# Last expert pair combined on chip by one-hot products, the other rows reloaded behind the last weights, and a reordered beginning

## What is computed

```python
for i in range(2):
    mod = silu(c) @ w_ada[i] + b_ada[i]              # 6 vectors of 1024, for both token groups
    x = x + mod[2] * mixer_i(rmsnorm(x, norm_mix[i]) * (1 + mod[1]) + mod[0])
    h = rmsnorm(x, norm_ffn[i]) * (1 + mod[4]) + mod[3]
    # each token goes to 2 of 32 experts (top group of 4, then top 2 of its 8), with gates g0, g1
    y = sum(g_c * (silu(h @ w_gate[e_c]) * (h @ w_up[e_c])) @ w_down[e_c] for c in (0, 1))
    x = x + mod[5] * y
out = rmsnorm(x, norm_final)
```

## Time and profile before

| what | before |
|---|---|
| median of three runs | 1372.38 us (1372.12 to 1373.4) |
| profiled execution: own time, span of its instructions | 1375.31 us, 1373.4 us |
| PE busy, DVE busy, ACT busy, POOL busy | 1208.0, 451.8, 329.9, 200.1 us |
| mean granted TensorE clock | 0.953 |
| DMA moved | 336.90 MB, mean 245 GB/s |
| chain that ended last | PE 68%, DMA 18%, DVE 6%, ACT 3%, POOL 2%, issue 2% |

### The profile page before, as it was taken

How to read it: one execution, slowest core, us unless ns; L and a number is a source line. 1 busy time by engine, 2 the same in 40 slices (tenths; PEclk the granted TensorE clock), 3 DMA queues, 4 the chain that set the end, 5 groups by cost and what they waited for, 6 DMA issues and landing times.

```text
span 1373.4 us, 16614 instructions
## 1 busy us (share of the span) xinstructions
PE 1208.0 (88%) x6373; PEld 679.4 (49%) x6373; DVE 451.8 (33%) x973; ACT 329.9 (24%) x843; POOL 200.1 (15%) x261
## 2 busy tenths in 40 slices
PE   3999998999989999959999774999888959989774
PEld 2456654554545554446555332753554446545431
DVE  1442078543238750331111104112364331111105
ACT  4112364300123200321111104213353321111103
POOL 1000012200124510011212101052001011212100
PEclk9999999999999999979999996999999979999996
DMA  9896510576920137369999996860314469999983
GB/s 338 307 386 228 184 31 1 197 266 222 359 78 1 62 127 266 103 232 420 419 415 420 419 373 227 304 64 0 138 63 140 178 231 420 420 418 420 419 371 148
DMA packets 94386, 336.90 MB, mean 245 GB/s; under 512 B 12769, under 2 KB 16583, under 8 KB 69618
## 3 DMA queue, kind: packets, MB, share of 16 engines
q1 hardware_dynamic: 73472, 303.18, 56.7%
q0 software_dynamic: 13952, 25.86, 6.8%
q10 hardware_dynamic: 6897, 6.97, 1.5%
HBM read 333.76 MB, written 23.18 MB: 260 GB/s over the span
## 4 chain that ended last, share of the span: by engine, by line
PE 68%; DMA 18%; DVE 6%; ACT 3%; POOL 2%; issue 2%; SPq 0%; ACTq 0%; DVEq 0%; POOLq 0%
PE bank L856 60%; DMA ring<-in_moe_w_down_dram 11%; PE bank L860 5%; DMA ring<-in_moe_w_up_dram 3%; PE bank L887 3%; DMA arena<-expert_rows 1%; DMA xR<-in_x_sample_dram 1%; POOL ring L2671 1%; POOL hT L2674 1%; PE bank L953 1%; ACT ring L1976 1%; DMA hT<-rows,scr 0%; POOL arena L2674 0%; DMA arena<-in_hy_freq_dram 0%; ACT rstd L1604 0%
## 5 line engine op out<-in xcount | busy, mean ns | idle before, releaser
L856 PE MATMUL bank<-ring,arena 128*64 128x256 f32 (+3 forms) x2624 | 440.3, 440 | 45.8 <-DMA ring<-in_moe_w_up_dram 17.2
L856 PEld LDWEIGHTS bank<-ring,arena 128*64 128x64 f32 (+1 forms) x2624 | 218.1, 146 | 232.4 <-issue 120.0
L856 PE MATMUL bank<-hT,ring 128*128 128x384 f32 (+4 forms) x960 | 302.7, 474 | 4.3 <-ACT hT L1676 3.6
L856 PEld LDWEIGHTS bank<-hT,ring 128*128 128x128 f32 (+1 forms) x960 | 179.2, 194 | 123.8 <-issue 16.6
L856 PE MATMUL bank<-arena 128*64 128x256 f32 (+7 forms) x800 | 118.0, 385 | 10.5 <-DVE arena L2459 4.5
L2486 DVE TENSOR_TENSOR hT<-hT,bank 128x256 f32<-128x256 f32 x32 | 13.5, 421 | 266.1 <-ACT hT L1863 266.1
L856 PEld LDWEIGHTS bank<-arena 128*64 128x64 f32 (+4 forms) x800 | 60.1, 151 | 52.3 <-issue 29.0
L1863 ACT ACTIVATE hT<-bank 128x256 f32<-128x256 f32 x32 | 12.3, 383 | 247.7 <-PE bank L856 247.7
L860 PEld LDWEIGHTS bank<-cst,hT 128*128 128x128 f32 x368 | 47.4, 190 | 48.1 <-issue 35.9
L860 PE MATMUL bank<-cst,hT 128*128 128x128 f32 x368 | 61.1, 301 | 11.4 <-DMA hT<-rows,scr 11.4
L860 PE MATMUL bank<-cst,arena 128*128 128x128 f32 (+3 forms) x207 | 32.6, 307 | 40.0 <-ACT arena L1617 23.4
(11 more groups left out here) (312 smaller groups left out, 1126.4 us busy)
## 6 DMA issues: line engine op xcount, KB each, us to landing
ring<-in_moe_w_up_dram SPq DMA_DIRECT2D x28, 2048.0 KB, 21.1
ring<-in_moe_w_down_dram SPq DMA_DIRECT2D x28, 2048.0 KB, 20.0
ring<-in_w_ada_dram SPq DMA_DIRECT2D x24, 2048.0 KB, 15.0
ring<-in_moe_w_gate_dram SPq DMA_DIRECT2D x24, 2048.0 KB, 21.1
ring<-in_ev_w_in_dram SPq DMA_DIRECT2D x11, 2048.0 KB, 11.7
arena<-in_moe_w_gate_dram SPq DMA_DIRECT2D x8, 2048.0 KB, 14.4
ring<-in_ev_w_out_dram SPq DMA_DIRECT2D x4, 2048.0 KB, 16.8
arena<-in_moe_w_up_dram SPq DMA_DIRECT2D x4, 2048.0 KB, 20.7
```

The source lines that it names most:

```text
L856: return nc.tensor.matmul(out, lhsT, rhs, start=start, stop=stop_, skip_group_check=True)
```

## The change

At the end of each expert stage step 15 is neither stored nor reloaded. A second table `gtb` (72 more products beside `tbl`) gives the gate of each slot; POOL takes the column of the last step and builds three diagonal matrices of the choice 0 gates (`diag0`); DVE builds `last_pick`, a 128 by 384 matrix that has a slot's gate in its token's column. PE then forms for each tile and half `diag0[t] @ yg[t]` plus `last_pick @ ob` in one bank (`last`, 12 products of 128 by 512), which replaces ACT's `weigh`. Since some rows of `expert_rows` are now never written, SP fills all of them with zeros beforehand (`k_zero`, four copies DRAM to DRAM ahead of the first `wout` load). On PE `down` of step 14 and the four `gff` products move ahead of `gate_up` of step 15, and down 14 is loaded to `ahead[2]`, ahead of gate 15. `row_loads` waits for the stores up to step 14 alone, and the `od` loads no longer wait for `yg2`. ACT measures tile 2 before it modulates tile 0.

At the beginning the two condition rows are loaded and transposed first, the wait at `k == 1` goes, the first `xbc` block is loaded in two halves with two `w_ada` blocks between them, and PE's work is reordered: a `w_ada` block before the parameter rows, the second half of the token transposes after the first sums, and `first_x` started after each 128-row chunk (`FIRST_MOD`, `first_taken`).

```diff
...
+FIRST_MOD = {"act": [(c, t) for c in range(4) for t in (0, 2)], "dve": [(c, 1) for c in range(4)]}
...
+    job(("cond",), "act")
     for g in range(2):
         job(("adaw", 0, g), "none", ("ada", 0, g), ADA_BANK)
+        if g == 0:
+            for i in range(5):
+                job(("par", i), "act")
+            for t in range(NT):
+                job(("xn", "mix0", t, 0), "first")
         job(("adaw", 0, g + 2), "act", ("ada", 0, g + 2), ADA_BANK)
         job(("ada", 0, g + 2), "dve", None, ADA_BANK)
+        if g == 0:
+            for t in range(NT):
+                job(("xn", "mix0", t, 1), "first")
...
+                job(("gff", l, v, h), "weighed", None, (0, 1, 7, 2)[2 * v + h])
+        for t in range(NT):
+            for h in range(2):
+                job(("last", l, t, h), "dve", None, (3, 4, 5, 6, 3, 4)[2 * t + h])
...
+                sp.wait_ge(done, JOB[("gtb", l)] + 1)
...
-                with sp.Fori(4, r - 1) as i:
...
-                next_load(l, 2 * r - 3, 2 * r - 1, 1, PAIRS - 1, 2)
+                m = 2 * r - 4
+                for part in range(2):
+                    next_load(l, m, m + 2, 0, PAIRS - 2, part)
+                next_load(l, m - 1, m + 1, 1, PAIRS - 3, 2)
+                sp.wait_ge(S("down_done%d" % l), len(PLACES[2]))
+                sp.dma_start(halves(expert_place(2, 2)), expert_source(l, PAIRS - 2, 2)).then_inc(expert_sem(l, 2, 2), 16)
+                for part in range(2):
+                    next_load(l, m + 1, m + 3, 1, PAIRS - 1, part)
+                next_load(l, m + 1, m + 3, 1, PAIRS - 1, 2)
...
-                for b in range(2):
-                    sp.wait_ge(S("stored%d_%d" % (l, b)), 16 * r)
+                even, odd = sp.to_reg(16 * r), sp.to_reg(16 * r - 16)
+                sp.wait_ge(S("stored%d_0" % l), even)
+                sp.wait_ge(S("stored%d_1" % l), odd)
...
+            first_k = LOAD_AT[("xbc", 0)]
             for k in range(n1 - 1):
-                if k == 1:
-
-                    sp.wait_ge(S("rows_in"), 16 * sum(len(t) for t in ROWS))
-                    sp.wait_ge(S("small_in"), 16 * 2)
-                static_load(k, False)
+                if k == first_k:
+                    sp.dma_start(block_view(LOADS[k])[:, 0:4, :], block_source(LOADS[k])[:, 0:4, :]).then_inc(S("first_x_in"), 16)
+                else:
+                    static_load(k, False)
+                if LOADS[k + 1] == ("wout", 0):
+                    for l in range(2):
+                        for c in range(2):
+                            sp.dma_start(outs_d[l][c * T:(c + 1) * T, :], K["k_zero"]).then_inc(S("blank"), 16)
+                if k == LOAD_AT[("ada", 0, 3)]:
+                    sp.dma_start(block_view(("xbc", 0))[:, 4:8, :], block_source(("xbc", 0))[:, 4:8, :])\
+                        .then_inc(S("full%d" % first_k), 16)
...
-                sp.wait_ge(S("yg%d" % (NT - 1)), 16)
...
+            pe.wait_ge(S("cond_in"), 16 * 2)
+            ps = open_bank("cond")
+            tr(ps[:, 0:2 * KD], prow[0:2 * KD, 0, :]).then_inc(done, 1)
+            pe.wait_ge(S("silc"), 1)
+            first_ada_block(0, 0)
+            pe.wait_ge(S("rows_in"), 16 * (sum(len(t) for t in ROWS) - 2))
...
-            for h in range(2):
-                for t in range(NT):
-                    ps = open_bank("xn", "mix0", t, h)
-                    pe.wait_ge(S("xn%d" % h), t + 1)
-                    for c in range(4):
-                        last = tr(ps[:, cols(c)], xn["mix0"][:, t, cols(4 * h + c)])
-                    last.then_inc(done, 1)
-            pe.wait_ge(S("silc"), 1)
+            for t in range(NT):
+                first_scaled(t, 0)
+            first_ada_block(2, 1)
             pe.wait_ge(S("small_in"), 16 * 2)
...
+            first_ada_sums(0)
+            for t in range(NT):
+                first_scaled(t, 1)
+            pe.wait_ge(S("first_x_in"), 16)
             for c in range(4):
                 if c == 3:
-                    first_ada(1)
+                    first_ada_block(1, 0)
+                    first_ada_block(3, 1)
...
+                down(n - 1, 0, 2)
                 pe.sem_inc(done, 1)
                 pe.wait_ge(S("gff_in"), 16 * (l + 1))
...
                 for v in range(2):
                     for h in range(2):
                         ps = open_bank("gff", l, v, h)
                         mm(ps[:, :], ones[0:1, :], gff_row[:, v, wide(h)], True, True).then_inc(done, 1)
+                gate_up(n, 1)
+                turn_hidden(n, 1)
+                down(n, 1)
+                pe.wait_ge(s["hid"], 2 * r)
+                pe.wait_ge(s["ht_act"], 2 * r)
+                pe.wait_ge(S("last_slots"), 3 * l + 3)
+                pe.wait_ge(s["d_dve"], 2 * r)
+                for t in range(NT):
+                    for h in range(2):
+                        ps = open_bank("last", l, t, h)
+                        pe.wait_ge(S("yg0%d" % h if t == 0 else "yg%d" % t), 16 * (l + 1))
+                        if t == 1:
+                            pe.wait_ge(s["d_act"], 2 * r)
+                        mm(ps[:, :], diag0[:, t, :], yg[t][:, 0, wide(h)], True, False)
+                        pe.wait_ge(s["d_act"], 2 * r)
+                        mm(ps[:, :], last_pick[:, cols(t)], ob[:, wide(h)], False, True).then_inc(done, 1)
...
+                take_down(n - 1, 0, 16 * (r - 1))
                 take_gate(n, 1)
-                take_down(n - 1, 0, 16 * (r - 1))
                 take_hidden(n, 1)
...
                     for h in range(2):
                         act.wait_ge(S("xup"), 2 * NT * l + 2 * t + h + 1)
                         squares(t, h)
 
-                weigh(0)
-                weigh(1)
                 measure(0)
-                weigh(2)
                 if l == 0:
                     scale("mix1", 0)
                 measure(1)
                 if l == 0:
                     scale("mix1", 1)
+                measure(2)
+                if l == 0:
                     take_scaled("mix1", 0)
-                measure(2)
...
+                parts = rsc[:, 620:632].bitcast(BF16).rearrange("p (x n) -> p x n", x=4)
...
+                for c in range(2):
+                    for x in range(3):
+                        last = TT(rgate[:, c, :, :, x], ohs[:, c], over(parts[:, x, NT * c:NT * c + NT], E), mult)
+                last.then_inc(S("onehot"), 1)
+                full(dve, "gtb", l)
+                take(RED(gtab, bank("gtb", l)[:, 0:288].rearrange("p (r x) -> p r x", x=3), AX_X, add))
...
+                take_down(n - 1, 0, 16 * (r - 1))
                 take_up(n, 1)
-                take_down(n - 1, 0, 16 * (r - 1))
+                dve.wait_ge(S("last_slots"), 3 * l + 2)
+                TS(last_pick, slotrow, last_tok, last_gate, ALU.is_equal, mult)
                 take_down(n, 1, 16 * r)
...
+                        y = yg[t][:, 1, wide(h)]
+                        full(dve, "last", l, t, h)
+                        dve.wait_ge(S("yg0%d" % h if t == 0 else "yg%d" % t), 16 * (l + 1))
+                        summed = STT(out=y, in0=y, scalar=ysw[:, NT + t:NT + t + 1], in1=bank("last", l, t, h), op0=mult, op1=add)
+                        take(summed)
+                        took(dve, "last", l, t, h)
...
+                        weighed = TT(y, y, bank("gff", l, v, h), mult)
+                        weighed.then_inc(S("weighed"), 1)
+                        dve.wait_ge(S("weighed"), 2 * NT * l + 2 * t + h + 1)
+                        TT(xR[:, t, wide(h)], xR[:, t, wide(h)], y, add).then_inc(S("xup"), 1)
...
+                    pool.wait_ge(S("blank"), 16 * 4)
...
+                pool.wait_ge(S("down_done%d" % l), 8)
                 dma(gff_row, gates_d[l, 1].unsqueeze(0)).then_inc(S("gff_in"), 16)
                 if l == 1:
                     dma(gfin_row, A["norm_final"].unsqueeze(0)).then_inc(S("gfin_in"), 16)
+                took(pool, "gtb", l)
+                for dst, src in ((last_tok, tbli), (last_gate, gtab)):
+                    nc.gpsimd.tensor_copy(dst, src[:, bass.ds(2 * r - 1, 1)]).then_inc(S("last_slots"), 1)
+                for t in range(NT):
+                    last = nc.gpsimd.tensor_tensor(diag0[:, t, :], ident, ysw[:, t:t + 1].to_broadcast([P, P]), ALU.mult)
+                last.then_inc(S("last_slots"), 1)
                 for n in range(2):
                     scatter(2 * r - 4 + n, n)
-                for b in range(2):
...
+                n = 2 * r - 2
...
+                store(0)
```

More of the change, by code:

```diff
@@ L634, in build_kernel @@
         done = S("pe_done")
-        taken = {x: S(x + "_took") for x in ("act", "dve", "act_first", "dve_first")}
+        taken = {x: S(x + "_took") for x in ("act", "dve")}
         def full(eng, *name):
@@ L982, in _ @@
+            arrived(("xbc", 0))
             for c in range(4):
@@ L1650, in _ @@
             act.wait_ge(S("const"), 1)
+            full(act, "cond")
```

(5 more changed lines are left out.)

199 lines of the change are left out of this document (100 added, 99 removed).

## The result

The changed kernel takes 1377.3 us (median of 6, 1374.4 to 1377.48) against 1372.25 before (median of 6). The ratio is 1.0024, with an interval of 1.0013 to 1.0035: slower by 1.8 to 4.8 us, where 1363.7 and a gain of 8.7 were forecast. The profiled execution has a span of 1375.4 us and took 1377.43.

A forecast was written before the change was run, and what follows sets the result against it. Loads set the pace while expert weights come in, but not at the beginning and layer ends, where the change acts. −4.7 + 2 × 0.8 − 2.2 − 3.4 = −8.7 from 1375.3, less 2.9 for the median: 1363.7, range 1357 to 1371.

The forecast's parts named there:

- the four blank copies: Ahead of the `wout` loads: copies cost nothing, as the DMA queues there were taken to be nearly idle.
- POOL's own small loads: At the blank copies: if POOL's small loads were late behind them, 1 to 4 us; not counted in the sum.
- Beginning: Kernel start, reordered loads and PE work: second half's projection ends at 57.0 against 61.76; gain 4.7, bounds 1.3 to 7.4.
- Rival D: Beginning: small rows land later than 22 us behind the weight queue, some 10 us lost, 1378 in all; chance 0.04.
- rival F: Beginning: PE leaves each dozen transposes at half clock, costing 1.8 and 2.0 us, 1367.5 in all; chance 0.04.
- Start of the experts: Before the first `turn`: gate table's operations and 72 products add 0.8 us a layer, 1.6 in all, bounds 0 to 2.5.
- Ends: Expert stage ends, last pair combined on chip: gross gains 6.7 (layer 0), 4.4 (layer 1); net 3.4 and 2.2 us.
- the clock: Both layer ends: one half clock stretch on PE behind the one-row `gff` products, costing 1.7 us each, between 0 and 3.7.
- the rows: Layer 1 end: step 14's store waits for step 13's, so reloaded rows may come late; 0 to 1.8 us, taken 0.5.
- rival E: Both layer ends: step 14's rows reload late, first result 3 to 4 us later, 1367.5 to 1371; chance 0.12.
- rival C: Layer ends: PE at half clock through 12 last products; one layer 1370.5, chance 0.08; both 1376 to 1379, chance 0.06.
- ACT's order: End of layer 0: ACT measuring tile 2 before modulating tile 0 delays the next layer's start 1.6 us, bounds 0 to 2.3.

The follow-up runs named there:

- b3: Kernel before plus only the four blank copies ahead of the first `wout` load; 1382.12 against 1373.15 us, ratio 1.0063.
- e1: Changed kernel with the blank copies issued once the first filter products are through; 1367.77 us, ratio 0.9959 to the kernel before.
- b1: Kernel before with the new beginning alone; 1366.87 us against 1373.15, ratio 0.9952.
- e3: e1 with ACT's old order, modulating tile 0 ahead of measuring tile 2; 1367.12 us, ratio 0.9952 to the kernel before.
- c4: e1 with e2's early count, DVE's gate parts computed early and ACT's old order, `gff` staying behind `down` 14; 1363.08 us, ratio 0.9927 to the kernel before.
- c2: b1 run once more without an edit, for a second trace; 1364.28 us.
- e2: e1 with PE's step-count register load and waits for seven banks ahead of the gate table's products; 1366.45 us, ratio 0.9952 to the kernel before.
- c1: Kernel before run once more without an edit, for a second trace; 1370.5 us.
- c3: b1 plus the gate table computed but read by nobody, no blank copies; 1370.49 us, ratio 0.9978 to the kernel before.
- b2: Kernel before with all of the change except the new beginning, copies placed as in e1; 1374.77 us against 1373.15, ratio 1.0006.
- e6: e1 with the four `gff` products ahead of `down` 14 instead of behind it; 1367.54 us, ratio 0.9967 to the kernel before.
- e7: e1 with the edits of e2, e3 and e6 together, plus DVE's gate parts computed early; 1364.1 us, ratio 0.9938 to the kernel before.

## Why the prediction was wrong

**The step that failed** is the clause "the four blank copies lie ahead of `wout` where the DMA queues are nearly idle (78 and 1 GB/s): nothing". Its numbers are right and its place is wrong. The slices with 78 and 1 GB/s run from 378 to 446 us; the copies are issued at 337.7, into two slices with 222 and 359 GB/s and ahead of POOL's loads, one of which PE wants at 378. Idle time that comes after the deadline hides nothing. The prediction saw the danger ("POOL's own small loads there"), priced it at 1 to 4 us without a row for how long those loads took (9.0 for the one that counts) or how long before its use it landed (2.2), and gave it no chance among the rivals. It cost 8.6 us alone (b3) and 8.9 in the changed kernel (against e1, by the ratios). The load landed 16.7 instead of 9.0 after its issue; with 9.0 it would have been there 1.4 before PE came to it, and 7.7 − 1.4 = 6.3 is the idle time of the row (6.39). The products behind it then took 8.03 instead of 5.39, 2.6 us at half clock. None of the five rivals was this one.

The copies did not hold POOL's loads up directly: they had landed by 371 us, when these had hardly begun to move. They made the `wout` loads late, and from 370 to 384 us these and POOL's loads had 52.5% and 46.5% of the engines, where POOL's had all of them from 374 us on before. The Trainium skill, page DMA: Bandwidth & Descriptors, section Queues, rings and completion order, says that each DMA engine goes round between the queues that have work for it, one packet at a time; the two shares agree with that. No run moves the `wout` loads alone.

**Beginning**, −4.7 forecast, bounds 1.3 to 7.4: right. The changed kernel's trace has −4.5; by the means of the 10 traces with the new beginning and the 4 with the old it is −5.4, and b1 has −6.6 in time. The first block was at half clock, as assumed. Rival D (rows late) did not happen. As for rival F, the block behind the twelve transposes took 1.92 or 1.93 in seven of the ten traces, the changed kernel's among them, and 2.60 to 2.75 in three (b1, e3, c4; b1's second trace, c2, has 1.92), and the projection behind the other twelve began at full clock in all. The Trainium skill, page TensorE: Matmul & The Clock Gate, Part 4: PE-mode transpose, says that the clock's faster level does not engage for transposes; these traces do not bear that out as a rule for the products behind them.

**Start of the experts**, +0.8 each forecast: the mechanism right, the size too small. Over six traces with the table against five without it is 2.2 in layer 0 and 1.4 in layer 1. From the slot table's first product to the last of `gtb` it was 7.9 us (603.52 to 611.47) where the sum had 8.7, as DVE's six products took 0.2 each and not 0.35. What the sum left out is DVE's reduction, 0.5, and PE's register load of the number of steps with its bank waits, which stands behind the last table and had been hidden behind 5.7 us of waiting for the gather: 1.3 and 0.7 us in the changed kernel, 0.05 in e2. In layer 0 more of PE's next gate and up products were at half clock (9.95 us for 64 records in the changed kernel, 8.82 before).

**Ends**, 6.7 and 4.4 gross, 5.0 and 2.2 after the clock and, in layer 1, the rows: from the table, 47.5 to 43.3 and 46.5 to 42.9, so 4.2 and 3.6, means of six traces each (before, c1, b3, b1, c2, c3; after, e1, b2, e6, e2, e3). From the end of `down` 15 to the last addition the changed kernel has 16.5 and 16.1 us; the prediction's 15.6 is 15.5 when its terms are added up. The pitch, the order of landings and PE as the last to end were as forecast; the rows cost nothing, so rival E did not come, and the `last` records at 0.44 rule out rival C; the half clock stretch behind `gff` came in nine places of twelve and cost 8.81 − 7.13 = 1.7 in eight of them, as priced.

**ACT's order**, 1.6 forecast: right in kind, too small by the traces. The start of layer 1 went from 7.2 to 10.1, 2.9, of which the old order brought back about 2.3 (7.9, mean of e3, e7, c4). In the changed kernel PE stood idle until ACT was ready and then ran its 32 records in 6.57 instead of 5.13.

Together −5.4 + 8.9 + 3.6 − 7.8 + 2.9 = +2.2, against 1.8 to 4.8 measured. Without the copies it would be −6.7 (e1 has −5.6 in time), so the forecast of −8.7 would have been somewhat too good even then: the table's start and ACT's order cost 3.3 more than it had for them, and the beginning and the ends gave 1.3 more. What stays open is a rest of 1 to 2 us: by the traces the ends with table and start should be 1.3 better than nothing, in time they are 0.8 worse (b2, −0.4 to 2.1), and 0.9 by e1 and b1. As runs of one kernel differ by up to 8 us (the kernel before beside c3 and c4: 1370.84 with a granted clock of 0.957, 1378.76 with 0.952), and most kernels have one trace, no cause for it is claimed.

The chances do not quite add up either: the rivals that are slower, C in both layers and D, have 0.06 + 0.04 = 0.10, where the summary gives "slower" 0.08.

## What to carry to other kernels

A transfer is hidden only if the idle time lies between its issue and the deadline of everything queued behind it, and of everything that then meets what it pushed back: read the window up to the next DMA releaser, not the slice average, and put bytes that nobody wants soon behind that releaser. When work is put where an engine used to wait, also list the small instructions behind it (register loads, bank waits) that the wait had hidden. A wait removed at the end of a stage was paid for here in part by work added to its start; both lie on the same chain, and both belong in one sum, with the clock at which PE ran behind each.

## What the runs showed of the hardware

The four `gff` products, whose contraction is one row long, ran at 0.46 us a record after `down` in the changed kernel, in 3.69 us. Placed ahead of it (e6 and e7, both layers) they ran at 0.65 or 0.66, with the following `down` at 5.40 to 5.54 instead of 3.65. In the six kernels that have `gff` between `down` 14 and gate 15 (after, e1, e2, e3, b2, c4; two layers each), the gate and up products behind it took 8.81 or more in nine places and 7.13 in three (layer 0 of the changed kernel and of e1, layer 1 of e3), though PE counts as busy throughout. Nothing in the runs tells why these three were spared. PE at the end of layer 1 of the changed kernel (a stretch, busy times, clock, DMA share, GB/s):

```profile
1337.00:1338.00 1.00, 1.00 (x5) 0.24 (x5) 0.00 (x0) 0.00 (x0) 0.00 (x0) 1.00 0.81 336
1339.00:1340.00 1.00, 1.00 (x8) 0.62 (x6) 0.69 (x1) 0.60 (x1) 0.00 (x0) 0.50 0.64 270
```

PE is busy in both, and the granted clock has gone from 2.4 to 1.2 GHz between them: the first stretch lies in the last `gff` products, the second in the gate products, which use all 128 rows.
